# Attention on one core: heads of both parities alternate on TensorE, masks first and over the diagonal block only

## What is computed

```python
s_c = jnp.einsum('bgrqd,bgnd->bgrqn', qq, kc)              # 15 compressed keys
p_c = masked_softmax(s_c, cmp_end[None, :] <= tq[:, None])
o_c = jnp.einsum('bgrqn,bgnd->bgrqd', p_c, vc)
s_s = einsum(qq, k_sel); p_s = masked_softmax(s_s, kpos_s <= tq); o_s = einsum(p_s, v_sel)
s_w = einsum(qq, kwb);   p_w = masked_softmax(s_w, m_w);          o_w = einsum(p_w, vwb)
y = gates[..., 0:1] * o_c + gates[..., 1:2] * o_s + gates[..., 2:3] * o_w
```

## Time and profile before

| what | us |
|---|---|
| median of 3 runs | 1994.57 |
| lowest and highest run | 1993.65 and 1995.47 |
| profiled execution, span from its first to its last instruction | 1993.8 |
| TensorE busy | 1916.4 |
| VectorE busy | 1425.4 |
| ScalarE busy | 1140.3 |
| DMA traffic (506.78 MB in all, nearly all of it weights), mean | 254 GB/s |

### The profile page before, as it was taken

One profiled execution on the slowest core, in us unless ns is written; L12 is line 12 of the kernel. 1 busy time (PEld: TensorE's weight loads), 2 busy tenths in 40 slices (PEclk: granted clock), 3 DMA queues, 4 the chain that ended last, 5 costly groups with the idle time before them and its releaser, 6 DMA issues.

```text
span 1993.8 us, 27929 instructions
## 1 busy us (share of the span) xinstructions
PE 1916.4 (96%) x11075; PEld 1653.8 (83%) x11075; DVE 1425.4 (71%) x1197; ACT 1140.3 (57%) x965; POOL 0.2 (0%) x4
## 2 busy tenths in 40 slices
PE   7999998999989999997999999999999999999996
PEld 7998898999979988996787887878878788788784
DVE  4574477454465564567888888888888788888887
ACT  5444344343435343444777767777767777776774
POOL 0000000000000000000000000000000000000000
PEclk9899999999999999998999999999999999999998
DMA  7433344545435333443898998989989899898994
GB/s 316 170 136 128 121 188 153 206 169 195 184 127 211 135 142 116 166 156 144 304 369 302 371 366 305 364 315 362 362 312 365 323 343 372 303 367 340 336 365 162
DMA packets 36170, 506.78 MB, mean 254 GB/s; under 512 B 3984, under 2 KB 4112, under 8 KB 5264
## 3 DMA queue, kind: packets, MB, share of 16 engines
q1 hardware_dynamic: 35104, 500.16, 66.9%
q10 hardware_dynamic: 1008, 5.77, 0.7%
HBM read 504.86 MB, written 1.05 MB: 254 GB/s over the span
## 4 chain that ended last, share of the span: by engine, by line
PE 87%; DVE 6%; issue 4%; ACT 2%; DMA 1%; DVEq 0%; SPq 0%; ACTq 0%
PE PS L342 16%; PE PS L344 15%; PE PS L343 15%; PE PS L328 10%; PE PS L329 10%; PE PS L330 10%; PE PS L766 2%; DVE tmp L1544 2%; PE PS L726 2%; DMA raw<-wstream 1%; PE PS L469 1%; DVE w_lo L1097 1%; ACT w_hi L810 1%; PE PS L501 1%; PE PS L484 1%
## 5 line engine op out<-in xcount | busy, mean ns | idle before, releaser
L1097 DVE TENSOR_TENSOR w_lo<-raw,w_hi 128x2048 fp32r<-128x2048 f32 x473 | 1082.5, 2291 | 397.5 <-ACT w_hi L810 397.0
L810 ACT ACTIVATE w_hi<-raw 128x2048 fp32r<-128x2048 f32 x473 | 905.2, 1916 | 378.1 <-PE PS L344 262.4
L328 PE MATMUL PS<-xT_hi,w_hi 128*128 128x256 f32 x1456 | 424.0, 291 | 12.8 <-DVE w_lo L1097 5.6
L329 PE MATMUL PS<-xT_lo,w_hi 128*128 128x256 f32 x1456 | 416.9, 286 | 0.0
L330 PE MATMUL PS<-xT_hi,w_lo 128*128 128x256 f32 x1456 | 416.6, 286 | 0.0
L342 PE MATMUL PS<-w_hi,xT_hi 128*128 128x512 f32 x896 | 357.7, 399 | 1.5 <-DVE xT_lo L1534 1.5
L344 PE MATMUL PS<-w_hi,xT_lo 128*128 128x512 f32 x896 | 349.5, 390 | 0.0
L343 PE MATMUL PS<-w_lo,xT_hi 128*128 128x512 f32 x896 | 348.6, 389 | 0.0
L328 PEld LDWEIGHTS PS<-xT_hi,w_hi 128*128 128x128 f32 x1456 | 284.4, 195 | 24.5 <-issue 19.7
L329 PEld LDWEIGHTS PS<-xT_lo,w_hi 128*128 128x128 f32 x1456 | 284.7, 196 | 0.2
L330 PEld LDWEIGHTS PS<-xT_hi,w_lo 128*128 128x128 f32 x1456 | 284.3, 195 | 0.0
(11 more groups left out here) (241 smaller groups left out, 1412.6 us busy)
## 6 DMA issues: line engine op xcount, KB each, us to landing
raw<-wstream SPq DMA_DIRECT2D x237, 2048.0 KB, 7.9
soft<-ln ACTq DMA_DIRECT2D x4, 1024.0 KB, 6.3
X<-x SPq DMA_DIRECT2D x1, 1024.0 KB, 4.8
out<-X ACTq DMA_DIRECT2D x2, 512.0 KB, 2.7
cst<-consts SPq DMA_DIRECT2D x1, 890.5 KB, 11.1
sm<-small SPq DMA_DIRECT2D x1, 729.0 KB, 12.8
bufA<-router ACTq DMA_DIRECT2D x1, 512.0 KB, 3.5
rg<-constb SPq DMA_DIRECT2D x1, 335.0 KB, 11.5
```

What stands on the lines that cost most here:

```text
L328: mm(o, wh, rhs_hi[:, k, :], start=(k == 0), stop=False)
L329: mm(o, wh, rhs_lo[:, k, :], start=False, stop=False)
L810: activate(w_hi[:, at % RING], raw_half(at // 2 % RING, at % 2), ACT.Copy).then_inc(hi_done, 1)
L1097: v.tensor_tensor(w_lo[:, at % RING], raw_half(at // 2 % RING, at % 2), w_hi[:, at % RING], ALU.subtract).then_inc(lo_done, 1)
```

## The change

Only the order and extent of TensorE's instructions changes, in `scores` and `weighted`. In `scores` the masks of both parities come first, and then the heads of parity 0 and parity 1 in turn. In a full step of the second tile the mask now covers the diagonal block alone (the last 128 keys of each head) instead of all 256 keys. In `weighted` the key blocks of both parities come in turn, and then Vc for both. The number of instructions, the banks, the waits and the semaphore increments stay.

```diff
                     if kind == "cmp":
                         m = cmpb[:, qt, :].unsqueeze(1).broadcast_to([P, NH // 2, NC])
+                        o = [PS[:, SB + par, 0:8 * NH].rearrange("p (i n) -> p i n", n=16)[:, :, 0:NC]
+                             for par in range(2)]
                         for par in range(2):
-                            o = PS[:, SB + par, 0:8 * NH].rearrange("p (i n) -> p i n", n=16)[:, :, 0:NC]
-                            mm(o, identb, m, start=True, stop=False, skip_group_check=True)
-                            for i in range(NH // 2):
-                                last = mm(o[:, i, :], query(2 * i + par, qt), kcT[par * DH:(par + 1) * DH, i // 2, :],
+                            mm(o[par], identb, m, start=True, stop=False, skip_group_check=True)
+                        for i in range(NH // 2):
+                            for par in range(2):
+                                last = mm(o[par][:, i, :], query(2 * i + par, qt),
+                                          kcT[par * DH:(par + 1) * DH, i // 2, :],
                                           start=False, stop=(i == NH // 2 - 1), skip_group_check=True)
                     else:
                         w = (qt + 1) * P
-                        m = maskb[:, 2 * P - w:2 * P].unsqueeze(1).broadcast_to([P, 2, w])
+                        m = maskb[:, P:2 * P].unsqueeze(1).broadcast_to([P, 2, P])
+                        o = [PS[:, SB + par, :].rearrange("p (i k) -> p i k", i=2) for par in range(2)]
                         for par in range(2):
-                            o = PS[:, SB + par, :].rearrange("p (i k) -> p i k", i=2)
-                            mm(o[:, :, 0:w], identb, m, start=True, stop=False, skip_group_check=True)
-                            for i in range(2):
-                                last = mm(o[:, i, 0:w], query(NR * g + 2 * i + par, qt),
+                            mm(o[par][:, :, qt * P:w], identb, m, start=True, stop=False, skip_group_check=True)
+                        for i in range(2):
+                            for par in range(2):
+                                last = mm(o[par][:, i, 0:w], query(NR * g + 2 * i + par, qt),
                                           kT[par * DH:(par + 1) * DH, a, g, 0:w], start=False, stop=(i == 1),
                                           skip_group_check=True)
...
-                    for par in range(2):
-                        o = PS[par * DH:(par + 1) * DH, YB, 0:2 * P]
-                        for kb in range(qt + 1):
-                            last = mm(o, V[:, a, kb, g * DH:(g + 1) * DH], probT[:, kb * 512 + par * 256:kb * 512 + (par + 1) * 256],
+                    o = [PS[par * DH:(par + 1) * DH, YB, 0:2 * P] for par in range(2)]
+                    for kb in range(qt + 1):
+                        for par in range(2):
+                            last = mm(o[par], V[:, a, kb, g * DH:(g + 1) * DH],
+                                      probT[:, kb * 512 + par * 256:kb * 512 + (par + 1) * 256],
                                       start=(a == 0 and kb == 0), stop=False, skip_group_check=True)
-                        if a == 1:
-                            last = mm(o, Vc[:, g, :], cprobT[0:NC, (4 * par + 2 * g) * P:(4 * par + 2 * g + 2) * P], start=False,
+                    if a == 1:
+                        for par in range(2):
+                            last = mm(o[par], Vc[:, g, :],
+                                      cprobT[0:NC, (4 * par + 2 * g) * P:(4 * par + 2 * g + 2) * P], start=False,
                                       stop=True, skip_group_check=True)
```

## The result

The changed kernel takes 1960.2 us as the median of four runs (1959.1 to 1965.04), against 1994.11 us for the kernel before. The ratio is 0.9839 with a 95% interval of [0.9824, 0.9854]. The profiled execution has a span of 1959.4 us against 1993.8.

What follows compares the result with a forecast made beforehand. TensorE, 96% of the span busy, was taken as the bound. Savings of 10.8 + 11.0 + 5.8 + 4.2 = 31.8 us, with the clock 33.5, gave 1961.1 us, range 1957 to 1971.

Steps and rivals of the forecast that it cites:

- Weighted sums: Sums with a = 1: both parities' V before Vc, so the second parity adds 0.01 us; 10.8 us saved.
- Scores: Score groups, masks first and both 64-row places at once: second tile saves 11.0 us, first tile 5.8 us.
- Compressed: Compressed scores, 4 steps: 2.25 us becomes 1.21 with the parities overlapping and 0.08 for a mask; 4.2 us saved.
- bounds for no overlap: Scores if 64-row places run one after the other: second tile saves 4.1 us, first 2.3, compressed 0.6.
- first rival: Scores: 64-row places don't overlap at all, only masks first helps; 17.8 us gain, 1976.8 us; chance 0.13.
- second rival: Scores: weight loads of the two row places go one after the other; 24.7 us gain, 1969.9 us; chance 0.10.
- Strict order of starts: Score groups: parity 1 starts only with parity 0's second record; 3.0 us less gain, 1964.1 us; chance 0.05.
- The clock: Behind layer 0's compressed scores: the fall to half clock goes once that stretch is shorter; 1.7 us, the less certain term.
- Who is late next: Transposes at 113.45 us, fed by VectorE: 0.73 of 0.78 us cover used up, just holds; costed at nothing.
- slower rival: Paired tiles make the clock fall, 1.7 us a fall; with 22 new falls 2000.2 us; chance 0.02.

Runs made afterwards that it cites:

- same-place experiment: Changed kernel with all score matmuls on rows 0 to 63, parity 1 reading parity 0's operands; 1974.89 us, ratio 0.9906 to the kernel before.

## Why the prediction was right, and where it wasn't

- **The time.** 1961.1 us was forecast, 1960.2 measured, and 1960.18 again. The groups carry it: 31.8 us forecast, 32.7 measured. The other 1.7 us came out by luck, as told under the clock.
- **Weighted sums.** 10.8 us forecast, 10.8 measured in the groups. The term rested on rows that showed the arrangement itself.
- **Scores.** 11.0 forecast and 11.0 measured for the second tile (8 x 1.37 us). For the first tile 5.8 forecast and 6.6 measured. Seven groups give 0.74 us or more each; the first group of all stood partly at half clock before (2.67 us) and takes 1.37 now, which I had costed as a plain one. Compressed 4.2 and 4.4: the added mask costs 0.04 us, below the 0.08 I took. That two 64-row places overlap in loads and matmuls was an inference from the 64-column places; the changed kernel and the same-place experiment show it. The Trainium skill, page TensorEngine Tiling (Array Packing), section Tiling Modes, states it, and now the trace agrees: 1.07 us for eight records in two places, 1.92 in one. The bounds for no overlap, 1.41, 2.24 and 2.09 us, came out at 1.41, 2.24 and 2.05, so the first rival's arithmetic was right and its premise wrong. In the second rival, serial loads, the first tile would stand at 1.41 us; it stands at 0.97.
- **Strict order of starts.** Excluded: two starts in 0.04 us. The order of the program is not even needed up to four records a place. It matters beyond that, which I had not foreseen. The Trainium skill, page TensorE: Matmul & The Clock Gate, section Part 3: Packing small matmuls, has starts in strict program order; the kernel without alternation shows parity 1's records starting while three of parity 0 still wait, and the trace decides.
- **The clock, the step that failed.** "For this fall to go: 1.7 us" was right about the fall at 87 us: the clock is 1.00 from 83.69 to 258.4 us now. Its price was a little high, 1.5 us measured. As a term of the sum it was wrong, since I treated one fall as a property of the kernel and took the others as untouched, and each fall is one draw among several places where it can happen. Two new ones behind the waits on L1196 cost 2.9 us; three more stretches of half clock that the kernel before had are gone or shorter and gave 4.0 us; 0.9 us went elsewhere. That the whole comes to 1.7 us again, the size of the term, is luck. A fall more or less moves the time by 1.5 us, and the runs of the changed kernel lie up to 6 us apart.
- **Who is late next.** Forecast: 0.73 of the 0.78 us cover used, "it just holds". Measured: 0.05 us between operand and transposes, and 0.08 us lost, twice. No other new wait appeared in the token mixers.
- **The slower rival** did not come: paired groups left the clock alone (0 of 24 behind the short compressed groups, and full clock from 83.69 to 258.4 us).

## What to carry to other kernels

Group small matmuls by the shape of the array they use. A change of shape cost 0.15 us here, and work of another shape between them is what kept two half-size places from working at once. Within one shape the hardware paired the places by itself where each had at most four records in a row; longer rows are worth alternating, shorter ones are not. And read a part's gain from its groups in the timeline before the total: stretches of half clock hid 3.4 of 10.8 us in one kernel and all of 1.7 us in another.

## What the runs showed of the hardware that I had not expected

- Each place of the array took up to three waiting records before the next place was fed: parity 1 joined with the fifth record of parity 0 in a row of eight, and blocks of six records cost 0.22 us over blocks of four.
- The same wait of 2.47 us is followed by a fall of the clock in 10 cases and not in 8, and none of the edits touches the instructions around it.
- A contraction over 15 rows costs more than the same one padded with zeros to 128 rows, 1.16 against 1.01 us for the group, and the padded one keeps the shape of the sums before it.
